# A hybrid decoder layer on one core: the forget projection in four column groups, the new tokens' values computed once, the first expert's tokens awaited tile by tile

## The reference

```python
z = h @ lw['w_in']                     # x_rnn | q | k | v | forget logits (16 columns) | gates
logf = log_sigmoid(f_logit + b_forget)
# samples: past = 256 cached rows, 8 new rows
k_all, v_all = concat(cache_k[page_table], k), concat(cache_v[page_table], v)
ft = cumsum(concat(cache_logf, logf))
p = softmax(where(mask, q @ k_all.T / 8 + ft[past:] - ft, -inf))
y_attn = p @ v_all                     # cached part + new part
merged = sigmoid(g_a) * y_rnn + sigmoid(g_b) * y_attn
x = x + gate1 * rms_norm(merged @ w_out)
h2 = rms_norm(x) * (1 + scale2) + shift2
# experts: top 4 of 32 by router logits, tokens gathered per expert
act = clamped_swiglu(xb @ w_gate_up[e] + b_gate_up[e]);  y = act @ w_down[e] + b_down[e]
```

## Time and profile before

| what | value |
|---|---|
| median of 3 runs | 1348.05 us (1345.96 to 1350.09) |
| the profiled execution, its own time | 1342.12 us |
| its span | 1340.3 us |
| PE busy | 1278.1 us, 95% |
| DVE, ACT, POOL busy | 357.9, 218.9, 45.5 us |
| chain that ended last | PE 78%, DMA 19%, DVE 1% |
| expert loads, 2 MB each, median to landing | 21.8 us (gate and up), 21.9 us (down) |
| read from HBM | 485.86 MB, 366 GB/s over the span |

### The profile page before, as it was taken

How to read it: one execution, slowest core, us unless ns; L and a number is a source line. 1 busy time by engine, 2 the same in 40 slices (tenths; PEclk the granted TensorE clock), 3 DMA queues, 4 the chain that set the end, 5 groups by cost and what they waited for, 6 DMA issues and landing times.

```text
span 1340.3 us, 15181 instructions
## 1 busy us (share of the span) xinstructions
PE 1278.1 (95%) x6118; PEld 542.0 (40%) x6118; DVE 357.9 (27%) x749; ACT 218.9 (16%) x499; POOL 45.5 (3%) x93
## 2 busy tenths in 40 slices
PE   5999999999999999999999989999998999999897
PEld 2566466664453333333233333323323333333232
DVE  2541325776562021021212101121210122121002
ACT  1124424421220110111011001011100110110002
POOL 1100003020010000000000000000000000000000
PEclk9999999999989999999999999999999999999999
DMA  9847569689888999999999999999999999999994
GB/s 347 283 143 286 195 239 250 189 233 297 288 341 353 408 414 429 428 429 425 427 427 427 427 428 429 425 428 428 427 428 428 427 427 429 427 426 429 428 427 163
DMA packets 72720, 492.26 MB, mean 367 GB/s; under 512 B 12229, under 2 KB 25405, under 8 KB 44868
## 3 DMA queue, kind: packets, MB, share of 16 engines
q1 hardware_dynamic: 68708, 480.99, 88.7%
q0 software_dynamic: 3936, 10.21, 2.7%
HBM read 485.86 MB, written 5.32 MB: 366 GB/s over the span
## 4 chain that ended last, share of the span: by engine, by line
PE 78%; DMA 19%; DVE 1%; issue 1%; ACT 0%; SPq 0%; DVEq 0%; ACTq 0%
PE bank L1990 27%; DMA ring<-in_w_gate_up_dram 16%; PE bank L2018 11%; PE bank L1678 8%; PE bank L1705 5%; PE bank L1966 4%; PE bank L1941 4%; PE bank L1544 2%; PE bank L1666 2%; PE bank L1817 2%; PE bank L2001 2%; DMA ring<-in_w_in_dram 1%; PE bank L1618 1%; PE bank L1945 1%; PE bank L1792 1%; PE bank L1969 1%
## 5 line engine op out<-in xcount | busy, mean ns | idle before, releaser
L1990 PE MATMUL bank<-ring,hga 128*64 128x512 f32 x1024 | 236.2, 599 | 12.5 <-DMA ring<-in_w_gate_up_dram 12.5
L1990 PE MATMUL bank<-ring,work 128*64 128x512 f32 x992 | 231.3, 602 | 10.3 <-DMA ring<-in_w_gate_up_dram 5.1
L2018 PE MATMUL bank<-ring,work 128*64 128x512 f32 x1024 | 227.1, 593 | 5.9 <-DMA ring<-in_w_down_dram 5.9
L2018 PEld LDWEIGHTS bank<-ring,work 128*64 128x64 f32 x1024 | 72.8, 137 | 154.1 <-issue 141.2
L1990 PEld LDWEIGHTS bank<-ring,hga 128*64 128x64 f32 x1024 | 67.6, 136 | 157.1 <-issue 131.0
L1990 PEld LDWEIGHTS bank<-ring,work 128*64 128x64 f32 x992 | 66.2, 137 | 151.2 <-issue 135.5
L1454 DVE TENSOR_SCALAR work<-bank 128x512 f32<-128x512 f32 x32 | 22.1, 692 | 356.4 <-PE bank L1990 356.4
L1678 PE MATMUL bank<-hga,ring 128*128 128x320 f32 x384 | 106.1, 436 | 1.9 <-DMA ring<-in_w_in_dram 1.9
L877 ACT ACTIVATE work<-bank 64x512 f32<-64x512 f32 x60 | 35.5, 591 | 340.1 <-PE bank L2018 339.3
L1678 PEld LDWEIGHTS bank<-hga,ring 128*128 128x128 f32 x384 | 71.9, 190 | 36.7 <-issue 4.3
L1466 DVE TENSOR_TENSOR gbT<-gbT,bank 128x512 f32<-128x512 f32 x75 | 51.6, 688 | 111.3 <-PE bank L1966 76.0
(11 more groups left out here) (371 smaller groups left out, 875.6 us busy)
## 6 DMA issues: line engine op xcount, KB each, us to landing
ring<-in_w_gate_up_dram SPq DMA_DIRECT2D x126, 2048.0 KB, 21.8
ring<-in_w_down_dram SPq DMA_DIRECT2D x64, 2048.0 KB, 21.9
ring<-in_w_ada_dram SPq DMA_DIRECT2D x12, 2048.0 KB, 10.3
ring<-in_w_in_dram SPq DMA_DIRECT2D x12, 2048.0 KB, 11.2
ring<-in_cache_k_dram SPq DMA_DIRECT2D x64, 128.0 KB, 7.7
ring<-in_cache_v_dram SPq DMA_DIRECT2D x16, 512.0 KB, 9.9
ring<-in_w_out_dram SPq DMA_DIRECT2D x2, 2048.0 KB, 10.9
out_dram<-tok POOLq DMA_DIRECT2D x2, 1024.0 KB, 8.3
```

The costliest lines, as they stand in the source:

```text
L1990: last = mm(B[x + 2 * q][CAP * h:CAP * h + CAP, :], slots[:, k, CAP * x:CAP * x + CAP], units[k // 2][:, k % 2, 1024 * q + 512 * h:1024 * ...
L2018: last = mm(bank[CAP * j:CAP * j + CAP, :], actT[:, 4 * y + m, CAP * h:CAP * h + CAP], slot[:, m, 512 * j:512 * j + 512], start=(h == 0 an ...
```

## The change

Three edits.

**The forget projection.** Its weights move from `fr` into unused columns of `qT`, padded with zeros from 16 to 32 columns (one more memset on POOL, and SP's load of them now stands behind the wait for it). The 8 matmuls of job `f` are written as 2 steps of 4, each of the four going to another group of 32 columns with another part of the contraction. ScalarE copies the four partial sums (128 rows) to `fpart`. A new job `F`, placed behind the first four k jobs, is one matmul with `fold32`, which adds the four groups. The log values now start from `F`. All later jobs get a number higher by one, and so another bank.

**The samples' values.** `svalues` loses its third step. The probabilities of the new tokens go to `PTn`, which keeps them for all samples (in `fr`). Behind `svalues(7)` TensorE does `new_values`: 16 matmuls, one per head, 64 rows by 64 columns out, in bank 2. VectorE adds that bank to `qT` (512 columns) ahead of the two merge operations. SP's load g = 0 of expert 0, whose buffer holds `PTn`, now waits for `new_values` and is issued last of the four.

**The tokens' tiles.** Expert 0 no longer waits for all four evictions of the gather at its start, but for 2, 3 and 4 of them ahead of g = 0, 1 and 3. The gather's pieces lie in other banks (`GBANK`), in the order 0, 2, 6, 1 for the evictions.

```diff
-        wf = fr[:, 2688:2816].rearrange("p (k h) -> p k h", h=H)
+        wf = qT[:, 4:6, :].rearrange("p t n -> p (t n)")[:, 0:256].rearrange("p (k h) -> p k h", h=32)
+        fpart = qT[:, 6, :]
+        PTn = fr[0:NS, 600:600 + DB * 128].rearrange("p (b c) -> p b c", b=DB)
...
-        PLAN += four("k", 0) + [("a", 6)] + four("k", 1) + [("a", 7)]
+        PLAN += four("k", 0) + [("F", 0), ("a", 6)] + four("k", 1) + [("a", 7)]
...
-            eng.dma_start(wf, winv[:, :, FCOL:FCOL + H]).then_inc(s["small_in"], 16)
+            eng.wait_ge(s["rgw_zeroed"], 2)
+            eng.dma_start(wf[:, :, 0:H], winv[:, :, FCOL:FCOL + H]).then_inc(s["small_in"], 16)
...
-                for x, g in ((0, 3), (0, 0), (0, 1), (0, 2), (1, 0), (1, 1), (1, 3), (1, 2)):
+                for x, g in ((0, 3), (0, 1), (0, 2), (0, 0), (1, 0), (1, 1), (1, 3), (1, 2)):
...
                     if (x, g) == (0, 0):
-                        eng.wait_ge(s["sprobs_made"], DB)
+                        eng.wait_ge(s["sv_ps"], DB + 1)
...
+            eng.memset(wf[:, :, H:32], 0.0).then_inc(s["rgw_zeroed"], 1)
...
                 elif kind == "f":
+                    A_(fpart, ps[:, 0:T], ACT.Copy).then_inc(s["job_ev"], 1)
+                elif kind == "F":
                     eng.wait_ge(s["small_in"], 64)
                     A_(lfz, ps[0:H, 0:T], ACT.Identity, bias=bfg).then_inc(s["job_ev"], 1)
...
-                A_(PT2[0:NS, b % 2, 256:384], B[3][0:NS, 256:384], ACT.Copy).then_inc(s["sPT_ev"], 1)
+                A_(PTn[:, b, :], B[3][0:NS, 256:384], ACT.Copy).then_inc(s["sPT_ev"], 1)
...
-            for i, (m, bank) in enumerate(((0, 0), (4, 6), (2, 1), (6, 2))):
+            for i, (m, bank) in enumerate(((0, 0), (4, 2), (2, 6), (6, 1))):
...
             eng.wait_ge(s["job_ev"], len(JOBS))
+            eng.wait_ge(s["sv_ps"], DB + 1)
+            link(TTo(qT[:, :, SP_:T], qT[:, :, SP_:T], B[2][:, :].rearrange("p (t n) -> p t n", n=NS), ALU.add))
             link(STT(gbT[:, :, SP_:T], gbT[:, :, SP_:T], 1.0, qT[:, :, SP_:T], ALU.add, ALU.mult))
...
-                    for k in range(NT):
-                        last = mm(ps[0:H, 0:T], wf[:, k, :], hT[:, k, :], start=(k == 0), stop=(k == NT - 1))
+                    for k in range(2):
+                        for g in range(4):
+                            last = mm(ps[32 * g:32 * g + 32, 0:T], wf[:, 2 * g + k, :], hT[:, 2 * g + k, :], start=(k == 0), stop=(k == 1))
                     last.then_inc(s["job_ps"], 1)
+                elif kind == "F":
+                    eng.wait_ge(s["job_ev"], LAST["f"])
+                    mm(ps[0:32, 0:T], fold32[:, :], fpart, start=True, stop=True).then_inc(s["job_ps"], 1)
...
-                for j in range(NPG + 1):
+                for j in range(NPG):
                     for g in range(4):
...
+            def new_values():
+                eng.wait_ge(s["sscores_read"], 2 * DB)
+                for h in range(H):
+                    p, o = divmod(h, 2)
+                    c = 32 * (h % 4) + DS * (h // 4)
+                    last = mm(B[2][64 * o:64 * o + 64, NS * p:NS * p + NS].rearrange("p (b q) -> p b q", q=DS),
+                              tok[0:NS, 2, HD * h:HD * h + HD], PTn[:, :, c:c + DS], start=True, stop=True)
                 last.then_inc(s["sv_ps"], 1)
...
                 svalues(b)
+                if b == DB - 1:
+                    new_values()
...
-            GBANK = (0, 1, 6, 2)
+            GBANK = (0, 6, 2, 1)
...
             def opening(t, filled, units, combined):
-                eng.wait_ge(s["XT_made"], 2 * t + 4)
...
+                def first_filled(x, g):
+                    eng.wait_ge((gu_ahead if x else gu_in)[g], 16)
+                    if x == 0 and g in (0, 1, 3):
+                        eng.wait_ge(s["XT_made"], (2, 3, 0, 4)[g])
```

More of the change, by code:

```diff
@@ L317, in hybrid_layer @@
         CHUNKS += [woutv[:, :, 512 * i:512 * i + 512] for i in range(2)]
-        LAST = {k: max(i for i, j in enumerate(JOBS) if j[0] == k) + 1 for k in "v k x f q r i ga gb".split()}
+        LAST = {k: max(i for i, j in enumerate(JOBS) if j[0] == k) + 1 for k in "v k x f F q r i ga gb".split()}
         G_K, G_LF, G_ST, G_CF = 0, 6, 7, 9
@@ L413, in _ @@
             eng.dma_start(brow, b_router).then_inc(s["small_in"], 16)
-            eng.wait_ge(s["rgw_zeroed"], 1)
             for g, w in enumerate((rg_w_a, rg_w_x)):
@@ L755, in _ @@
                 job(j)
-                if j == LAST["f"]:
+                if j == LAST["F"]:
                     eng.wait_ge(s["absw_made"], 2)
@@ L1064, in _ @@
             w_, t_, x_ = lft[0:H, 1, 0:T], lft[0:H, 0, 0:T], lft[0:H, 2, 0:T]
-            eng.wait_ge(s["job_ev"], LAST["f"])
+            eng.wait_ge(s["job_ev"], LAST["F"])
             STT(t_, lfz, -1.0, lfz, ALU.mult, ALU.max).then_inc(s["absw_made"], 1)
@@ L1787, in svalues @@
                     eng.wait_ge(s["sy_read"], b)
-                for j in range(NPG + 1):
+                for j in range(NPG):
                     for g in range(4):
-                        n = 128 if j < NPG else NS
-                        vals = kv[:, b % 2, NPG + j, :] if j < NPG else tok[0:NS, 2, :]
                         last = mm(B[4][32 * g:32 * g + 32, 0:256].rearrange("p (h d) -> p h d", h=4),
-                                  PT2[0:n, b % 2, 128 * j + 32 * g:128 * j + 32 * g + 32],
-                                  vals.rearrange("p (h u d) -> p u h d", h=4, u=4)[:, g], start=(j == 0), stop=(j == NPG))
+                                  PT2[:, b % 2, 128 * j + 32 * g:128 * j + 32 * g + 32],
+                                  kv[:, b % 2, NPG + j, :].rearrange("p (h u d) -> p u h d", h=4, u=4)[:, g],
+                                  start=(j == 0), stop=(j == NPG - 1))
+                last.then_inc(s["sv_ps"], 1)
+            def new_values():
[5 more added lines that the diff above has]
+                              tok[0:NS, 2, HD * h:HD * h + HD], PTn[:, :, c:c + DS], start=True, stop=True)
                 last.then_inc(s["sv_ps"], 1)
@@ L2051, in first, with filled_again @@
             def first(t):
-                opening(t, lambda x, g: eng.wait_ge((gu_ahead if x else gu_in)[g], 16), gu_first, None)
-            def restart(t):
-                opening(t, lambda x, g: eng.wait_ge(gu_in[g], 32 * t + 16 * x), [gu_slot, gu_slot], t)
+                def first_filled(x, g):
+                    eng.wait_ge((gu_ahead if x else gu_in)[g], 16)
+                    if x == 0 and g in (0, 1, 3):
+                        eng.wait_ge(s["XT_made"], (2, 3, 0, 4)[g])
+                opening(t, first_filled, gu_first, None)
+            def restart(t):
+                def filled_again(x, g):
+                    eng.wait_ge(gu_in[g], 32 * t + 16 * x)
+                    if (x, g) == (0, 0):
+                        eng.wait_ge(s["XT_made"], 2 * t + 4)
+                opening(t, filled_again, [gu_slot, gu_slot], t)
             def pair(t, i, u, at):
```

## The result

The changed kernel took 1336.15 us (median of 7 runs, 1333.95 to 1340.93), the kernel before 1346.72 us beside it (7 runs, 1344.17 to 1351.13). The ratio is 0.9934, 95% interval [0.9915, 0.9953]: 6.3 to 11.4 us faster.

A forecast was written before the change was run, and what follows sets the result against it. It took the end to hang on the first expert's start, behind a TensorE chain and ahead of bandwidth-limited weight loads. Forget -2.38, samples -1.37 and tiles -0.98 summed to -4.73 us, giving 1343.3 us, range 1339 to 1347.3.

The forecast's parts named there:

- The forget projection: On TensorE's chain before the experts: job `f` falls from 4.29 to 1.22 us, plus a 0.69 fold, saving 2.38.
- Rival A: The forget projection's 2.38 us is swallowed by transfer waits among the samples; 2.35 us faster in all, 1345.7; chance 0.17.
- second excursion to 32-wide groups: At the forget projection: two changes to 32-wide groups instead of one, each draining TensorE; a drain of up to 0.15 us.
- The tiles: Ahead of the first expert: waiting for two evictions instead of four starts it 0.98 us sooner, bounds 0 and 2.10.
- rival C: Expert 0's first quarter, loaded last, arrives after TensorE is ready; slower, 1353 us; chance 0.03.
- VectorE's extra operation: Ahead of `merged`: one more 0.69 us operation, hidden by 2.27 us of cover before TensorE's projection.
- the term of the samples' values: Samples' stage: 2.22 us kept from dropping the third step, less 0.85 for `new_values`, net -1.37 us.
- The limit at sample 7's queries: Sample 7's scores need queries ready at 343.40, so at most 1.08 of the 1.71 us from samples 3 to 5 is kept.
- The third step: Last step of each sample's values on TensorE: 0.57 us, eight times, 4.6 us in all, not all kept.
- `new_values`: Behind the last sample's values: 16 small matmuls take 1.4 us, 0.55 of it in an existing wait, leaving +0.85.
- The savings of samples 0 to 2: Lost to waits for cached values: 1.14 us of samples 0 and 1, and sample 2's 0.57.
- rival B: TensorE's clock ahead of the experts: a third half-clock stretch, 1345.0 us, chance 0.09; one or two fewer, 1341.6 or 1339.9, 0.10.

The follow-up runs named there:

- e3: Only the forget projection changed, against the kernel before: ratio 0.9982 [0.9960, 1.0005].
- e8: The changed kernel with the first expert waiting for all four evictions as before, against the kernel before: ratio 0.9962 [0.9939, 0.9985].
- e15: The changed kernel with the samples' values as before (forget projection and tokens' tiles only), against the kernel before: ratio 0.9954 [0.9931, 0.9978].
- e11: The kernel before with the samples' values' third step made of 128 rows: third step and scores took 2.51 us for 2.78 with the values' other steps; no ratio.
- e14: The changed kernel again, unedited, against the kernel before: ratio 0.9951 [0.9929, 0.9972].
- e16: Only the samples' values changed, load order included, against the kernel before: ratio 0.9963 [0.9946, 0.9981].
- e6: Only the waits for the gathered tokens' tiles and the banks changed, against the kernel before: ratio 0.9997 [0.9975, 1.0019].
- e2: The kernel before, unchanged, timed against itself: ratio 1.0009 [0.9992, 1.0027].

## Why the prediction was wrong

**What held.** The end hangs on the first expert's start: the rest was 937.7 to 939.9 us in every trace. The forget projection came out as named, 2.69 for 2.38, 2.69 kept up to the prompt's first scores. Rival A, that it is lost among the samples, is not borne out: e3 alone, 0.9982 [0.9960, 1.0005], can't say, but the fit's 2.7 +- 1.9 excludes no gain, if narrowly. The price of 1.22 us had been read from a row that contains a change of shape. The new job follows a piece of the same shape and takes 1.08, and the fold stands ahead of one, so the change makes no second excursion to 32-wide groups, which the prediction had feared. The tiles gave 0.89 for 0.98. The quarter that is loaded last was in time (rival C), and VectorE's extra operation was covered.

**The step that failed** is the term of the samples' values, -1.37 us. The runs give 3.5 +- 1.4. In the profiled pair, from sample 3's values to `sfold(7)`, before 321.56 to 365.96 and after 320.05 to 361.83, the change saves 44.40 - 41.78 = 2.62. Three numbers in the term were off, all one way. The limit at sample 7's queries cost 0.63 in the sum; in this pair it never bound, for the keys landed 3.0 us sooner, where I had held their landing fixed. The limit itself is real: in e8, the change without T, these scores waited 0.59 us. SP's issue of these keys, before and after:

```profile
320.53 5.63 SPq L448 DMA_DIRECT2D ring<-in_cache_k_dram  x8
```

```profile
319.19 4.45 SPq L450 DMA_DIRECT2D ring<-in_cache_k_dram  x8
```

1.3 of the 3.0 us is the earlier issue, behind work that moved too; why the way to landing was shorter by the rest stays open. The third step was priced from start to start at 0.57, which leaves the switch back, paid by the scores, out: 0.13 for each of the three samples with scores behind them. `new_values` took 1.08 for 1.4. That is 0.63 + 0.39 + 0.32 = 1.34, where the difference between 2.62 and 1.37 is 1.25. What lies between the pair's 2.62 and the fit's 3.5 is not shown; the paragraphs on samples 0 to 2 and on the clock say where it can be.

**What stayed as forecast, with a doubt.** The savings of samples 0 to 2 were not kept in the profiled pair: from sample 0's scores to sample 3's values 38.47 us before and 39.05 after. Over the other traces with the loads in their places this stretch goes from 36.6 to 43.5 us, so one pair does not say it for the mean. From sample 0's values to sample 3's the seven traces with the third step average 29.1 us and the six without it 27.9, each with a standard deviation of 2 to 3 us: some 1.2 us may be kept, and nothing is shown. Nor was it all waiting, since in the pair TensorE's lower clock behind sample 2's wait took 1.69 us (3.84 for 2.15).

**The pair step by step**, to the end: start of the forget job +0.61, forget -2.69, up to sample 3 +0.58, samples 3 to 7 -2.62, up to the first expert -0.99, rest -0.78; together -5.9. The forecast for this execution was -4.7. The step of -0.99 holds the tiles' 0.89. The first, +0.61, is not the change but the clock; the chains of before and after at the first projection jobs:

```profile
37.60 18.33 PE bank L1678 x64
```

```profile
37.38 19.16 PE bank L1689 x64
```

The same 64 instructions took 0.83 us more, and the clock granted from 38.1 to 41.5 us was 0.50 after and 1.00 before.

**The range.** It was drawn around a median of three runs, 1348.05, and one profiled pair. Single runs scatter with 3.2 us, the mean of before is 1345.9, 2.1 lower, and the profiled execution of before was a quick one, 3.8 below that mean. Of the 7.1 us between the forecast 1343.3 and the measured 1336.15, the anchor was too high by 2.1, the sum too small by 3.2, and 1.8 is the luck of seven runs, whose median lies below the mean of 1338.0. The chance of 0.53 for faster was right in sign.

**The clock**, rival B, moved little in the mean: granted were 0.9908 of full speed over 137 runs of before and 0.9915 over the changed kernel's 31. Among the 137 runs, 0.001 less goes with 1.1 us more (correlation -0.61), so the difference is worth some 0.8 of the 7.9 us, an estimate. In the profiled pair it worked against the change. Ahead of the first expert the changed kernel had four times 3.4 us at 0.50, before had two:

```profile
38.10:41.50 3.40, 3.40 (x8) 2.16 (x7) 3.26 (x15) 0.00 (x0) 0.00 (x0) 0.50 0.99 390
311.20:314.60 3.40, 3.40 (x32) 1.53 (x24) 0.42 (x1) 0.00 (x0) 0.00 (x0) 0.50 1.10 240
365.80:372.60 6.80, 6.80 (x20) 2.77 (x21) 5.86 (x17) 1.59 (x5) 1.47 (x2) 0.50 0.96 406
```

The last of these costs what the two of before cost, 3.3 us against the same groups of matmuls at full clock. The first took 0.83 us. Of the second's 1.69 only 0.7 count, since sample 3's values landed at 319.4 (issued at 306.81, 12.6 to landing) and TensorE began them at 320.1. Without both, the pair's -5.9 would be -7.4, an estimate from these rows and near the 7.9 of the means: most of what the pair lacks looks like the clock of that one execution. The clock also makes long runs long. The windows of e15 (F and T), columns as in the earlier trace rows: a wait of 2.91 us ahead of sample 2's values, and the lower clock for the 10.2 us behind.

```profile
308.00:311.20 3.20, 1.05 (x4) 0.38 (x3) 1.39 (x5) 0.61 (x2) 0.00 (x0) 1.00 1.13 212
311.30:321.50 10.20, 9.54 (x65) 4.79 (x66) 4.49 (x11) 1.19 (x4) 0.00 (x0) 0.50 1.08 253
```

From there to sample 3's values took 12.58 us (311.96 to 324.54), against 8.58 before (312.98 to 321.56, wait included): 4.0 us more in a stretch with one wait and the lower clock behind it. The clock fell after a stretch with little work, 1.05 us in 3.2, and stayed low while TensorE was busy 9.54 of 10.2 us. The Trainium skill (TensorE: Matmul & The Clock Gate, What's actually happening) has activity release the throttle; the fall agrees with that, the 10.2 us under work do not show it.

## What to carry to other kernels

Where one stage is paced by transfers and feeds a long stretch at the bandwidth limit, a saving on TensorE is worth what is kept at the start of that stretch; read it as the time from there to the end, which was constant within 2.2 us here while whole runs scattered over 16. A wait for a load is not a wall at a fixed time: what releases the load moves too, so give such a term both ends. A profile is one execution: read the stretches at the lower clock in both, and price them, before a difference of a few us is put down to the change. Price a removed matmul group from the start before it to the start after the next group, for a change of array shape is paid by the neighbour.

## What the runs showed of the hardware

A change of TensorE's shape from 128 by 32 to 64 by 32 and back costs 0.27 us (e11). Eight 32-bit matmuls of 320 columns in four column groups take 1.08 us behind work of the same shape, and 1.21 to 1.22 behind wider work or 64 rows. In the samples' stage the transfer engines are busy (share 1.05) at 287 GB/s, where the 2 MB loads later reach 425: by share alone the queue looks as full in both. A kernel on one core scattered by 3.2 us with full transfers there (144 runs); the ten runs with thin ones scattered by 1.7. How long TensorE waited does not say whether its clock falls: behind waits of 1.96 (e14) and 2.62 us (e16) it stayed at 1.00, behind 2.34 (e6) and 2.91 us (e15) it was 0.50 for 10.2 us, behind 4.50 us (e2) for 3.4. The Trainium skill (TensorEngine Tiling (Array Packing), Key Properties) says that a change of the tiling mode drains TensorE; these rows agree that a change costs time, 0.13 to 0.14 us each.
